# Routing of a two-choice expert layer: where the tiles' transposes, logits and expert choices run

## The reference

```python
u = rmsnorm(h, norm_ffn_g)
g_logits = u @ w_group + b_group                     # 4 groups
p_grp, g_sel = top_k(softmax(g_logits), 1)           # one group
e_logits = (u @ w_router + b_router).reshape(n, 4, 8)
in_grp = e_logits[chosen group]                      # 8 experts
p_exp, e_sel = top_k(softmax(in_grp), 2)             # two of them
gate = p_grp * p_exp / sum(p_exp)
expert = g_sel * 8 + e_sel
```

## Time and profile before

| | us |
|---|---|
| median of 3 runs (2331.75 to 2332.29) | 2332.2 |
| the profiled execution, whole time | 2332.89 |
| its span, first to last instruction | 2331.1 |
| PE busy | 2172.8 |
| DVE busy | 990.1 |
| output stage (from 1736.2 to 1811.7) | 75.5 |
| routing, barrier to first expert product (1811.7 to 1835.9) | 24.2 |
| experts and the final sum (from 1835.9) | 495.2 |

### The profile page before, as it was taken

One profiled execution on the slowest core, in us unless ns is written; L12 is line 12 of the kernel. 1 busy time (PEld: TensorE's weight loads), 2 busy tenths in 40 slices (PEclk: granted clock), 3 DMA queues, 4 the chain that ended last, 5 costly groups with the idle time before them and its releaser, 6 DMA issues.

```text
span 2331.1 us, 25184 instructions
## 1 busy us (share of the span) xinstructions
PE 2172.8 (93%) x9688; PEld 1451.1 (62%) x9688; DVE 990.1 (42%) x1993; ACT 434.4 (19%) x818; POOL 108.1 (5%) x139
## 2 busy tenths in 40 slices
PE   8999999999989999999999999899999988777786
PEld 6888888545657788888764666556875433222232
DVE  6555444124777554543443246867641400000014
ACT  2010000145362110100021113552112000000001
POOL 0000000000101000000020000210000000000000
PEclk9999999999999999999999999999999998998999
DMA  5132232311021322322124122001242899999997
GB/s 160 55 99 83 73 100 82 105 36 36 1 91 65 99 91 73 106 98 86 64 63 106 36 73 68 5 12 55 82 164 119 330 423 427 427 427 427 426 381 311
DMA packets 173722, 347.50 MB, mean 149 GB/s; under 512 B 18099, under 2 KB 144179, under 8 KB 153138
## 3 DMA queue, kind: packets, MB, share of 16 engines
q1 hardware_dynamic: 167536, 331.66, 38.3%
q0 software_dynamic: 5504, 12.32, 1.5%
q10 hardware_dynamic: 578, 2.10, 0.2%
HBM read 337.33 MB, written 16.26 MB: 152 GB/s over the span
## 4 chain that ended last, share of the span: by engine, by line
PE 70%; DMA 17%; DVE 6%; issue 3%; ACT 2%; DVEq 1%; SPq 1%; ACTq 0%; POOL 0%; POOLq 0%
PE PS L636 19%; DMA M<-w 11%; PE PS L667 10%; PE PS L3443 7%; PE PS L73 6%; PE PS L2791 5%; DMA M<-w_ffn_up 4%; PE PS L2964 2%; PE PS L1000 2%; PE PS L415 2%; PE PS L1576 1%; PE PS L1948 1%; PE PS L1027 1%; PE PS L970 1%; PE PS L337 1%
## 5 line engine op out<-in xcount | busy, mean ns | idle before, releaser
L636 PE MATMUL PS<-M 128*128 128x256 f32 x2464 | 537.1, 380 | 3.3 <-DMA M<-w_ffn_up 1.4
L636 PEld LDWEIGHTS PS<-M 128*128 128x128 f32 x2464 | 466.6, 190 | 74.5 <-DMA M<-w_ffn_up 8.9
L3443 PE MATMUL PS<-M 128*64 128x512 f32 x1536 | 361.9, 630 | 84.0 <-DMA M<-w 60.9
L3443 PEld LDWEIGHTS PS<-M 128*64 128x64 f32 x1536 | 114.1, 145 | 319.3 <-issue 216.6
L667 PE MATMUL PS<-M 128*128 128x256 f32 x1232 | 268.7, 379 | 5.5 <-DVE M L825 3.1
L667 PEld LDWEIGHTS PS<-M 128*128 128x128 f32 x1232 | 233.4, 190 | 42.6 <-issue 11.3
L3543 DVE TENSOR_TENSOR M<-M,PS 128x512 f32<-128x512 f32 x16 | 11.0, 687 | 410.2 <-PE PS L3443 410.2
L762 DVE TENSOR_TENSOR M<-M,PS 128x256 f32<-128x256 f32 x220 | 92.6, 421 | 200.1 <-PE PS L636 195.7
L73 PE MATMUL PS<-M 128*128 128x264 f32 (+1 forms) x486 | 158.3, 484 | 0.6 <-ACT M L314 0.6
L2791 PE MATMUL PS<-M 128*128 128x256 f32 x616 | 134.9, 380 | 3.8 <-DVE M L2891 1.8
L2791 PEld LDWEIGHTS PS<-M 128*128 128x128 f32 x616 | 115.8, 190 | 22.5 <-DVE M L2891 2.3
(11 more groups left out here) (401 smaller groups left out, 2267.8 us busy)
## 6 DMA issues: line engine op xcount, KB each, us to landing
M<-w SPq DMA_DIRECT2D x128, 1024.0 KB, 19.1
M<-w SPq DMA_DIRECT2D x32, 2048.0 KB, 24.3
M<-w_ffn_gate SPq DMA_DIRECT2D x22, 1024.0 KB, 5.4
M<-w_ffn_up SPq DMA_DIRECT2D x22, 1024.0 KB, 5.3
M<-w_ffn_down SPq DMA_DIRECT2D x16, 1024.0 KB, 5.1
M<-w_in SPq DMA_DIRECT2D x27, 512.0 KB, 3.8
M<-w_in SPq DMA_DIRECT2D x12, 1024.0 KB, 5.3
M<-w_ffn_down SPq DMA_DIRECT2D x8, 768.0 KB, 4.4
```

The costliest lines, as they stand in the source:

```text
L636: last = nc.tensor.matmul(PS[:, 3 * half + BANK[p], 0:HALF], lhs[:, a, :], rhs[:, a, :], start=p in FIRST and a == 0, stop=p in LAST and a ...
L3443: last = nc.tensor.matmul(PS[ROWS * k:ROWS * k + ROWS, bank, :], wide[:, a * P + ROWS * k:a * P + ROWS * k + ROWS], weights(k), start=star ...
```

## The change

- **PE.** Tile t is turned behind job (t+1, 0) instead of behind (t+1, 1), and its logits are issued in the middle of job (t+1, 1), after four of its eight products. After the last job only turn(3) and logits(3) are left. The semaphores `ut_ready` and `ut_out` now count half tiles, and the logits of a tile start when its first half has been copied out.
- **DVE, output stage.** After tiles 0 to 2, `choose_dve(0, 3)` chooses the experts of these three tiles, before `turned(3)` and `normed(3)`. So the norm of the last tile now stands behind both.
- **DVE, routing stage.** `choose_dve(3, 1)` does the last tile alone. The choice itself has another form: a row of 40 holds the 32 expert logits, the 4 group logits and 4 fillers; as five rows of eight it gives the best of every group and the best group at once (five steps), and again with the best ones taken out (one and five steps). E12 is then the product of the group's one-hot and the experts'. The number of the chosen expert takes three steps more (BY_GROUP, sum, combination), and the two subtractions for the gates move from ahead of L3260 to behind L3282, with two steps more (BY_GROUP, sum) between them.
- **Layout.** The router columns and biases change places (experts first).

```diff
@@ out_pe
                 for a in range(KD):
+                    if half == 1 and t > 0 and a == KD // 2:
+                        logits(t - 1)
                     nc.tensor.matmul(PS[:, n % 2, :], ZT[:, a, lo:lo + P], WO[:, a, 512 * half:512 * half + 512],
                                      start=a == 0, stop=False)
...
             for n, (t, half) in enumerate(HN_JOBS):
                 pe.wait_ge(hn_free, n + 1)
                 rows(n, t, half)
-                if half == 0 and t >= 2:
-                    logits(t - 2)
-                if half == 1 and t >= 1:
+                if half == 0 and t >= 1:
                     turn(t - 1)
             turn(NT - 1)
-            logits(NT - 2)
             logits(NT - 1)
@@ out_dve
-            for t in range(NT):
-                if t == NT - 1:
-                    turned(NT - 2)
-                    turned(NT - 1)
+            def normed(t):
                 dve.wait_ge(rs5, t + 1)
                 nc.vector.scalar_tensor_tensor(UN[t], HN[:, t, :], C5["rs"][:, t:t + 1], GROW,
                                                ALU.mult, ALU.mult).then_inc(un_ready, 1)
-                if 0 < t < NT - 1:
-                    turned(t - 1)
+
+            for t in range(NT - 1):
+                normed(t)
+                turned(t)
+            choose(0, NT - 1)
+            turned(NT - 1)
+            normed(NT - 1)
@@ new
+        def choose_dve(dve, lo, n):
...
+            nc.vector.memset(LG[:, tiles, 36:40], -BIG)
+            dve.wait_ge(lg_ready, lo + n)
+            for t in range(lo, lo + n):
+                ins = stt(LG[:, t, 0:36], PS[:, 6, 36 * t:36 * t + 36], C5["rs"][:, t:t + 1], g["router_bias"], ALU.mult, ALU.add)
+            then(ins)
+            order = over(C["g8"], 5 * n)
+            for j, logits in enumerate((LG, LG2)):
+                values, dest = by_eight(logits[:, tiles, :]), by_eight(CHOICE[:, j, tiles, :])
+                best, place = flat(BEST[:, j, tiles, :]), flat(PLACE[:, j, tiles, :])
+                then(nc.vector.reduce_max(best, values, axis=AX))
+                then(tt(dest, values, bc(best, 8), ALU.is_equal))
+                then(tt(dest, dest, order, ALU.mult))
+                then(nc.vector.reduce_max(place, dest, axis=AX))
+                then(tt(dest, dest, bc(place, 8), ALU.is_equal))
+                if j == 0:
+                    then(stt(by_eight(LG2[:, tiles, :]), dest, -BIG, values, ALU.mult, ALU.add))
+            for j in range(2):
+                ins = tt(E12[:, j, tiles, :].rearrange("p t (g e) -> p t g e", g=4),
+                         CHOICE[:, 0, tiles, 32:36].unsqueeze(3).to_broadcast([P, n, 4, 8]),
+                         CHOICE[:, j, tiles, 0:32].rearrange("p t (g e) -> p t g e", g=4), ALU.mult)
+            then(ins)
+            ins = tt(ES[:, tiles, :], E12[:, 0, tiles, :], E12[:, 1, tiles, :], ALU.add)
+            if lo + n == NT:
+                ins.then_inc(routing_given, 1)
@@ route_dve
+            choose_dve(dve, NT - 1, 1)
...
+            then(tt(BY_GROUP, PLACE[:, :, :, 0:4], by_choice_group, ALU.mult))
+            then(nc.vector.reduce_sum(by_choice(C10["eid"]), BY_GROUP, axis=AX))
+            then(stt(by_choice(C10["eid"]), PLACE[:, 0, :, 4].unsqueeze(1).to_broadcast([P, 2, NT]), -8.0,
+                     by_choice(C10["eid"]), ALU.mult, ALU.subtract))
...
-            tt(GE, G, bc(C5["gmax"], 4), ALU.subtract).then_inc(choice_in, 1)
-            tt(C5["ex"], C5["m2"], C5["m1"], ALU.subtract).then_inc(choice_in, 1)
...
+            tt(GE, LG[:, :, 32:36], bc(BEST[:, 0, :, 4], 4), ALU.subtract).then_inc(choice_in, 1)
+            then(tt(BY_GROUP, BEST[:, :, :, 0:4], by_choice_group, ALU.mult))
+            then(nc.vector.reduce_sum(by_choice(C10["top"]), BY_GROUP, axis=AX))
+            then(tt(C5["ex"], C10["top"][:, NT:2 * NT], C10["top"][:, 0:NT], ALU.subtract)).then_inc(choice_in, 1)
             dve.wait_ge(choice_out, 1)
```

More of the change, by code:

```diff
@@ L3085, in mix2_dve @@
             gates_dve(dve); stage(dve, "dve")
-            out_dve(dve); stage(dve, "dve")
+            out_dve(dve, lambda lo, n: choose_dve(dve, lo, n)); stage(dve, "dve")
         RG0 = WS0
@@ L3110, in small @@
             return at(sc0[0] - n, *shape, dt=dt)
[L3112 to L3114 removed]
+        LG, LG2 = small(NT, 40), small(NT, 40)
+        CHOICE = small(2, NT, 40)
+        BEST, PLACE, BY_GROUP = small(2, NT, 5), small(2, NT, 5), small(2, NT, 4)
+        GE = small(NT, 4)
         T96, E12 = at(RG0 + 4096, 2, NT, 32), at(RG0 + 4416, 2, NT, 32)
@@ L3118, in program @@
         BE = [small(32), small(32)]
-        C5 = {n: small(NT) for n in ("gmax", "gsum", "mx", "m1", "m2", "ex", "den", "ga1", "ga2", "ss", "rs")}
-        C10 = {n: small(2 * NT) for n in ("rank", "pair", "half", "ob", "q", "in", "eid", "step", "last")}
+        C5 = {n: small(NT) for n in ("gsum", "ex", "den", "ga1", "ga2", "ss", "rs")}
+        C10 = {n: small(2 * NT) for n in ("rank", "pair", "half", "ob", "q", "in", "eid", "step", "last", "top")}
         LAST_PAIR = small(1)
@@ L3198, in route_pe, with then, by_eight, flat @@
             transpose_rows(pe, 16)
+        def choose_dve(dve, lo, n):
+            tiles = slice(lo, lo + n)
+            def then(ins):
+                dve.drain()
+                return ins
+            tt, stt = nc.vector.tensor_tensor, nc.vector.scalar_tensor_tensor
+            def by_eight(ap):
+                return ap.rearrange("p t (g e) -> p (t g) e", e=8)
+            def flat(ap):
+                return ap.rearrange("p t g -> p (t g)")
+            nc.vector.memset(LG[:, tiles, 36:40], -BIG)
[22 more added lines that the diff above has]
+                ins.then_inc(routing_given, 1)
         def route_dve(dve):
@@ L3206, in route_dve @@
             tt, ts_, stt = nc.vector.tensor_tensor, nc.vector.tensor_scalar, nc.vector.scalar_tensor_tensor
-            dve.wait_ge(lg_ready, NT)
-            for t in range(NT):
-                stt(LG[:, t, :], PS[:, 6, 36 * t:36 * t + 36], C5["rs"][:, t:t + 1], g["router_bias"], ALU.mult, ALU.add)
             nc.vector.memset(ES[:, NT, :], 0.0)
[L3211 to L3234, removed]
             ts_(STEP64, C["iota"][:, 1:9], float(ROWS), None, ALU.mult)
-            dve.drain()
-            tt(ES[:, 0:NT, :], E12[:, 0], E12[:, 1], ALU.add).then_inc(routing_given, 1)
+            choose_dve(dve, NT - 1, 1)
+            group = CHOICE[:, 0, :, 32:36]
+            by_choice_group = group.unsqueeze(1).to_broadcast([P, 2, NT, 4])
             def by_choice(column):
```

27 lines of the change are left out of this document (12 added, 15 removed).

## The result

The changed kernel takes 2335.6 us against 2332.4 (medians of 20 runs each): ratio 1.0014, 95% interval 1.0009 to 1.0020, or +3.3 us with 2.1 to 4.7. The forecast was +2.2 us, 2334.4. So it is slower, clear of scatter, but by less than the 0.2% up to which the forecast counted a time as the same.

What follows compares the result with a forecast made beforehand. The expert weight stream, waiting on the first gather's landing, was taken to bound the kernel. A count 1.8 us later plus names 0.36 later gave +2.2 us on the 2332.2 median, 2334.4 us; range 2331.2 to 2336.5.

Steps and rivals of the forecast that it cites:

- The end of the last job: PE, output stage: turn(2) and logits(2) now stand ahead of the last job's end, which comes 2.60 us later.
- The barrier: Between output and routing stage: passed 2.0 us later, ended by DVE's last norm and ACT's store instead of PE.
- The choice of three tiles: DVE ahead of turned(3): takes 5.3 us, or 6.3 at the upper price, hidden with 0.4 to 1.2 us to spare.
- Rival C: DVE ahead of turned(3): the choice of three tiles holds DVE up, slower by over 0.2%, 2338.2 us; chance 0.05.
- The choice of the last tile: DVE behind the barrier: choosing only the last tile takes 4.0 us instead of 7.13.
- The dummies: PE behind the barrier: 12 dummy instructions take 7.0 us at a fallen clock, so the count starts 1.8 us later.
- rival A: PE behind the barrier: dummies run at full clock, count +0.2 us, end +0.6, 2332.8 us; chance 0.2.
- Rival B: Barrier and PE: the barrier isn't later or the dummies don't hold PE; -0.8 us, 2331.4 us; chance 0.08.
- The gate steps: DVE between count and gather: moved and added gate steps make the names 0.36 us later, bounds 0 to 0.8.
- The gather: First gather of rows: meets no more traffic than before, so it adds nothing; stream and end follow its landing.
- The sum: Gather, weight stream and end: +1.8 and +0.36 give +2.2 us, median 2334.4 us; chance 0.62.
- The upper end of the range: Terms reach +3.3 us (dummies 7.2, gates 0.8, cut jobs 0.3), plus 1 us for the late hole: 2336.5 us.

Runs made afterwards that it cites:

- dummies4: Changed kernel with four dummy products ahead of the token count instead of six; count 4.01 us after the barrier, no ratio given.
- dummies8: Changed kernel with eight dummy products ahead of the token count instead of six; count 9.35 us after the barrier, no ratio given.
- after_again: Second profile of the unaltered changed kernel; count 7.40 us after the barrier, first gathered rows landed 28.57 us after the last job's copy.
- two_early: Kernel before with the new choice form, tiles 0 and 1 chosen early, four dummies, some gate steps behind the names; ratio 0.9994 to the kernel before.
- two_early_again: two_early measured and profiled once more, unaltered; ratio 0.9999 to the kernel before.
- form_best: form_only with four dummy products instead of six and the four gate steps back ahead of the wait for stored rows; ratio 0.9997 to the kernel before.
- store_first: The kernel both with the last tile's store on SP's queue ahead of the 2 MB, instead of on ACT's; ratio 1.0008 to the kernel before.
- norm_late: Changed kernel with the last tile's norm and store moved from ahead of the barrier to the routing stage's head; ratio 1.0011 to the kernel before.
- both: norm_late with the four gate steps also put back ahead of the wait for stored rows; ratio 1.0020 to the kernel before.
- before: First profile of the kernel before the change, unaltered; median 2332.4 us.
- before_again: Second profile of the unaltered kernel before; first gathered rows landed 27.81 us after the last job's copy.
- order_only: Kernel before with only the new PE order, half-tile semaphores and turned(3) ahead of normed(3), old choice form; ratio 1.0009 to the kernel before.
- form_only: Changed kernel with the old PE and DVE output order, all four tiles chosen behind the barrier in the new form; ratio 1.0000 to the kernel before.

## Why the prediction was right, and where it wasn't

The mechanism came out in its main step, the later barrier that takes back the shorter choice. Two of its terms, the dummies and the gather, did not come out, and their errors partly cancel, so that the total comes closer than the reasons deserve.

- **The end of the last job.** +2.60 forecast, +2.66 and +2.67 measured. Cutting logits into a job cost nothing that shows.
- **The barrier.** +2.0 forecast, +2.2 measured from the first product (77.73 - 75.51). ACT's root and DVE's norm end it, as said; moving the norm took 1.50 off it. The 0.2 is what lies between the store's issue and the barrier, 0.58 us, where I had 0.44, and the 0.06 of the last job.
- **The choice of three tiles.** Priced at 5.3, it took 5.7 (1805.98 to 1811.69); one gap of 0.42 between two steps, where the others have 0.07, is most of the difference. A step of 120 elements takes 0.28 and begins 0.36 after the last, which is the price taken. It was hidden, with 1.14 us to spare. Rival C is out.
- **The choice of the last tile.** 4.0 forecast, 3.94 and 3.96 measured.
- **The dummies.** 7.0 taken, between 5.4 and 7.2. Measured were 5.25 and 7.40: a term that has two values, and I had put the chance of the lower one at 0.2, while five of eight profiles with the new order had it. I had written that I am wrong if the clock stays at 1.00 through the dummies. It did in the first profile of the changed kernel, so there this step failed and the condition of rival A held; in the second it was as forecast. The reason I gave, that little work ahead of the dummies makes the clock fall, doesn't decide it: the same work stood ahead of them both times. That the dummies hold the count is shown by dummies4 and dummies8. Rival B, by which they don't, is out.
- **The gate steps.** +0.36 forecast for the names. From the take-up to the names it is 8.09 and 8.10 instead of 7.69: +0.4.
- **The gather.** I had it meet no more traffic than before and take as long as before: nothing in the sum. It took 4.28 and 4.34 us instead of 3.55 and 3.64, **0.7 us that the forecast lacks**. At full clock it did meet the last of the 4 MB (DMA share 0.99 in the microsecond before its issue, 0.72 in the one after). But that isn't shown to be the cause: after_again took as long with the engines idle before it (0.04), and two_early took 3.77 with as much beside it (0.99 and 0.76). All seven profiles that have both the new order and the new form took 4.25 to 4.73; of the other seven six took 3.55 to 3.82, and two_early_again 4.47. Why is open.
- **The sum.** With the 2.66, the first rows land 1.3 and 3.4 us later than in the kernel before (26.35 and 28.57, against 27.71 and 27.81), 2.4 in the mean, where 2.2 was forecast. That agreement is partly luck: in the mean of the two the count came 0.5 us earlier than forecast (+1.3 instead of +1.8), and the gather's 0.7 filled the place. The end followed the landing, 497.3 and 499.7 us behind it against 496.1 and 497.8 before. The measured difference is 3.3 with 2.1 to 4.7. Whether the rest, about 1 us, belongs to the change or to where the clock falls in the first expert, 13.95 to 16.9 us of products, my few profiles can't tell. It stays open. The upper end of the range has a slip: 7.2 for the dummies, 0.8 and 0.3 add up to +3.1 and not +3.3, which decides nothing here.

Why nothing was gained is then this. The choice behind the barrier became 3.2 us shorter, but the barrier came 2.2 us later, since the work moved ahead of the last job's end delays the root and the norm behind it. Of the 3.2 the count kept only 1.9 where the clock stayed full, and nothing (0.2 later) where it fell, because the dummies then end last. Behind the count the gate steps cost 0.4 and the longer gather 0.7. That makes +1.3 us at full clock and +3.4 at the low one.

## What to carry to other kernels

Work that is moved off a path into an engine's earlier stream is free only if it isn't moved ahead of that stream's last result: here the 2.60 us of products put before the end of the last job delayed the root and the norm that hang on it by 2.66. Before a step is shortened, list what ends near it (here the dummy products, within 0.1 us) and price each against the new end. When filler work is taken away, look at what it was hiding: in form_best and store_first DVE's own 2.6 us then came last. In this case a small store that others wait for was best issued ahead of a large load.

## What the runs showed of the hardware

- A 512 KB store issued 1.4 us behind a 2 MB load on another queue landed 8.2 us after its issue in norm_late and 8.6 in the kernel both; issued 0.55 us ahead of the load it took 2.9 in the changed kernel, and ahead of it on the same queue 2.9 in store_first.
- The same twelve 512-column instructions, behind the same 36-column products and idle time, held the count for 5.25 us with the clock at 1.00 and for 7.40 with the clock at 0.50 from 1812 to 1816. The clock had fallen ahead of the dummies in one execution (0.50 in the 2 us before the barrier) and not in the other (1.00). The Trainium skill ("TensorE: Matmul & The Clock Gate", section on the HAM clock gate) says that the point at which the clock goes back up in sustained work varies from run to run. What varied in these two profiles is more than that: whether there was a low stretch here at all.
- The first gather of 128 rows of 4 KB took 3.55 to 3.82 us in five profiles with the DMA engines nearly idle in the last microsecond before it (share 0.04 to 0.08; before, before_again, order_only, form_only, form_best), but 4.29 in dummies8 and 4.34 in after_again with them just as idle (0.00 and 0.04). What separates these isn't shown.
